# Three attention blocks on TensorE issued one projection unit later, each beside its neighbour (hybrid decoder layer, one core)

## The chip, the cores and the metric

The kernel runs on one core of one Trainium2 chip. The metric is the device time of one execution in microseconds (us), the median of several. PE is TensorE's matmul stream, PEld its weight loads, DVE VectorE, ACT ScalarE, POOL GpSimd, SP the engine that issues most of the DMAs.

## What is computed

One decoder layer over 512 positions of width 2048 in float32: RMSNorm, a combined input projection, two attention groups side by side, an output projection, then a SwiGLU feed-forward block and a final RMSNorm. Only the attention with the projections around it matters here:

```python
h = rmsnorm(x, attn_norm)
proj = einsum('bsd,de->bse', h, w_in)        # qa, ka, va (16 heads), qb (16 heads), kb, vb (2 kv heads)
out_a = dilated_attention(qa, ka, va)        # (window, dilation) = (128,1), (512,4), (2048,16), merged
out_b = swa_sink_attention(qb, kb, vb)       # window 128, learned sinks, 8 query heads per kv head
mix = concat(rmsnorm(out_a), rmsnorm(out_b))
x = x + mix @ w_out
x = x + (silu(h2 @ w_gate) * (h2 @ w_up)) @ w_down      # h2 = rmsnorm(x)
```

## The kernel before

Every engine runs its own instruction stream, written out by hand, and the streams meet only in counting semaphores. Float32 products are made of two fp32r halves: a tensor is split into a high part (ACT, `..._hi`) and the rest (DVE, `..._lo`), and three products of halves are added in PSUM.

**Units.** The projection is cut into units. A unit is one 128x512 tile of weights, times h, 12 matmuls of 512 columns (`tall_unit`, L445 to L447, in a loop of four). A pass `pair(p, ...)` has 16 units: four each for q, k, v of group A and q of group B of head pair p. Behind unit number s of the pass PE issues `attend(s, a, kv)`, a piece of the attention of the pair before (a = p - 1). So attention is laced into the projection, and a unit between two pieces is the time in which the other engines answer the first. There are 8 such interlaced passes: pair(1), a loop over pairs 2 to 4, a loop over pairs 5 to 7, and the output projection's first 16 units (`out_unit`, L489 to L491, also 12 matmuls each), which carries the attention of pair 7.

**Attention of a pair** has four heads, h = 0 and 1 of group A (dilated), h = 2 and 3 of group B. For each:
- `scores` (L592, L593) makes blocks of q times k. For a head of group A the last block, `S_A[3:]`, uses bank 2 again and so waits until ACT has read the first block (`exp_done`).
- DVE adds the bias and takes row minima (`lows`, L1307), ACT takes exponentials (`exps`, L848), DVE the reciprocals of the sums, POOL scales the rows.
- `turn_p(a, h, r)` (L608) transposes the probabilities of round r into the one bank BANK_PT. ACT takes their high part (`pt_high`, L860), DVE the low part (`pt_low`, L1259). As there is one bank, each `turn_p` waits until the round before has its low part (`pt_lo_done`).
- `weigh_v(a, h, r)` (L624, L625) multiplies round r with v into BANK_O. After a head's last round ACT copies one half of that bank (`o_lower`, L869), and DVE adds the two halves (`take_o`, L1334).
- `turn_v` (L632) transposes v for the pair.

Heads 0 and 1 have three rounds, heads 2 and 3 two. ACT and DVE step through the same 16 numbers: each first splits the weights three units ahead (`split`: w_hi L805 on ACT, w_lo L1250 on DVE; ACT's waits until the unit four before has been used), then does its own piece. At step 12 these pieces read, word for word:

```python
# ACT, attend(s, a)
            if s == 12:
                o_lower(a, 1)
                pt_high(a, 2, 0)
# DVE, attend(s, a)
            if s == 12:
                denominators(a, 3)
                take_o(a, 1)
                pt_low(a, 2, 0)
```

The low part's wait and the bank's wait are `pe.wait_ge(pt_lo_done, ROUNDS * a + r0 + r)` in `turn_p`, where r0 is 0, 3, 6, 8 for the four heads and ROUNDS is 10.

Of the kernel before, what the change touches and what calls it, by code (L numbers as in the profile page):

```python
# [99 lines left out]
def build(nc, x, x_turned, gain_cols, w_in, sinks, w_out, w_gate, w_up, w_down, final_norm, c_dist, c_lnm, c_band, c_slope, c_ident, x_mid, gu_mid, out):  # L100
# [341 lines left out]
    def _(pe):  # L442
# [143 lines left out]
        def scores(a, h, blocks):  # L586
            kind, odd, _ = HEAD[h]
            q, kh, kl = q_both[kind][odd], k_both[kind][odd], k_lo[kind][odd]
            for b, bk, c0, k0, keys, _ in blocks:
                qs, ks, s = slice(P * b, P * (b + 1)), slice(k0, k0 + keys), bank[bk][:, c0:c0 + keys]  # L590

                nc.tensor.matmul(s, q[:, qs], kh[:, ks], start=True, stop=False, skip_group_check=True)  # L592
                nc.tensor.matmul(s, q[:, qs], kl[:, ks], start=False, stop=True,  # L593
                                 skip_group_check=True).then_inc(s_ready, 1)

        def turn_p(a, h, r):

            kind, _, r0 = HEAD[h]
            if r == 0:
                pe.wait_ge(p_ready, 16 * a + 4 * (h + 1))  # L600
            if not (isinstance(a, int) and a == 0 and r0 + r == 0):
                pe.wait_ge(pt_lo_done, ROUNDS * a + r0 + r)
            where = E_A if kind == "A" else E_B
            for kb, qbs, c0 in (PT_A if kind == "A" else PT_B)[r]:
                for n, qb in enumerate(qbs):
                    e, k0 = where[qb]
                    e += P * kb - k0
                    mm = nc.tensor.transpose(bank[BANK_PT][:, c0 + P * n:c0 + P * (n + 1)],  # L608
                                             probs[h % 2][:, e:e + P], ident[:, :])
            mm.then_inc(pt_ready, 1)  # L610

        def weigh_v(a, h, r):

            kind, odd, r0 = HEAD[h]
            rounds = PT_A if kind == "A" else PT_B
            pe.wait_ge(pt_lo_done, ROUNDS * a + r0 + r + 1)
            if r == 0 and h > 0:
                pe.wait_ge(o_taken, 4 * a + h)
            buf = (r0 + r) % 2
            for i, (kb, qbs, c0) in enumerate(rounds[r]):  # L620
                n = P * len(qbs)
                v = v_both[kind][:, kb, 2 * odd:2 * odd + 2, :].rearrange("p a d -> p (a d)")
                o = bank[BANK_O][:, P * qbs[0]:P * qbs[0] + n]
                nc.tensor.matmul(o, v, pt_hi[:, buf, c0:c0 + n], start=r == 0 and i == 0, stop=False, skip_group_check=True)  # L624
                mm = nc.tensor.matmul(o, v, pt_lo[:, buf, c0:c0 + n], start=False,  # L625
                                      stop=r == len(rounds) - 1 and i == len(rounds[r]) - 1, skip_group_check=True)
            mm.then_inc(pv_done, 1)

        def turn_v():

            for t in range(NT):
                mm = nc.tensor.transpose(bank[BANK_O][:, P * t:P * (t + 1)], proj[0][:, P * t:P * (t + 1)], ident[:, :])  # L632
            return mm

        def attend(s, a, kv):

            first = isinstance(a, int) and a == 0
            if s == 0:
                pe.wait_ge(qa_lo_done, 2 * (a + 1))
                pe.wait_ge(ka_lo_done, 2 * (a + 1))  # L640
                pe.wait_ge(ka_hi_done, 4 * (a + 1))
                if first:
                    pe.wait_ge(k_rest_zero, 4)
                if not first:
                    pe.wait_ge(exp_done, 16 * a)
                scores(a, 0, S_A[:3])
            if s == 1:
                pe.wait_ge(exp_done, 16 * a + 1)
                scores(a, 0, S_A[3:])
            if s == 2:  # L650
                pe.wait_ge(acc_taken, 5 + 4 * a)
                if first:
                    pe.wait_ge(vb_all_done, 1)
                else:
                    pe.wait_ge(o_taken, 4 * a)
                turn_v().then_inc(vt_ready, 1)
            if s == 3:
                pe.wait_ge(exp_done, 16 * a + 4)
                scores(a, 1, S_A[:3])
            if s == 4:  # L660
                turn_p(a, 0, 0)
                pe.wait_ge(exp_done, 16 * a + 5)
                scores(a, 1, S_A[3:])
            if s == 5:
                turn_p(a, 0, 1)
                pe.wait_ge(va_lo_done, a + 1)
                weigh_v(a, 0, 0)
            if s == 6:
                turn_p(a, 0, 2)
                weigh_v(a, 0, 1)  # L670
                pe.wait_ge(qb_lo_done, 2 * (a + 1))
                pe.wait_ge(kb_lo_done, 2 * (kv + 1))
                pe.wait_ge(exp_done, 16 * a + 8)
                scores(a, 2, S_B)
            if s == 7:
                weigh_v(a, 0, 2)
            if s == 8:
                turn_p(a, 1, 0)
            if s == 9:
                turn_p(a, 1, 1)  # L680
                weigh_v(a, 1, 0)
                pe.wait_ge(exp_done, 16 * a + 12)
                scores(a, 3, S_B)
            if s == 10:
                turn_p(a, 1, 2)
                weigh_v(a, 1, 1)
            if s == 11:
                weigh_v(a, 1, 2)
                turn_p(a, 2, 0)
            if s == 12:  # L690
                turn_p(a, 2, 1)
            if s == 13:
                pe.wait_ge(vb_lo_done, 2 * (kv + 1))
                weigh_v(a, 2, 0)
                turn_p(a, 3, 0)
            if s == 14:
                weigh_v(a, 2, 1)
                turn_p(a, 3, 1)
            if s == 15:
                weigh_v(a, 3, 0)  # L700
                weigh_v(a, 3, 1)

        def pair(p, a, kv):

            for c, b in enumerate((BANK_Q, BANK_K, BANK_V, BANK_K)):

                if c == 0 and a is not None:
                    pe.wait_ge(acc_taken, 4 * p - 1)
                if c == 3 or c == 1 and a is not None:
                    pe.wait_ge(acc_taken, 4 * p + c + 1)  # L710
                if c == 2 and a is not None:
                    pe.wait_ge(acc_taken, 4 * p + 1)
                for j in range(4):
                    tall_unit(U_PAIR // 4 + 4 * p + c, j, b, h_hi, h_lo)
                    if a is not None:
                        attend(4 * c + j, a, kv)
                    if a is None and c == 1 and j == 2:
                        pe.wait_ge(ident_loaded, 16)
                        spread_r(squares[:, :].rearrange("p (t c) -> p t c", c=P), 1, BANK_PT)
                    if a is None and c == 2 and j == 0:  # L720
                        pe.wait_ge(acc_taken, 2)
                        turn_v().then_inc(vbt_ready, 1)
# [14 lines left out]
        for g in range(2):  # L737
            for s in range(16):
                out_unit(g, s)
                if g == 0:  # L740
                    attend(s, PAIRS - 1, 1)
                if g == 1 and s == 2:

                    pe.wait_ge(sq_added, 2 * PAIRS)
                    pe.wait_ge(pt_lo_done, ROUNDS * PAIRS)
                    for i, kind in enumerate("AB"):
                        for t in range(NT):
                            mm = nc.tensor.matmul(bank[BANK_PT][:, 4 * i + t:4 * i + t + 1],
                                                  sq_sum[kind][:, P * t:P * (t + 1)], ones[:, 0:1], start=True, stop=True)
                    mm.then_inc(ssq_ready, 1)  # L750
# [1128 lines left out]
```

## Time and profile before

| what | value |
|---|---|
| time, median of 3 runs | 2032.45 us (2032.43 to 2033.32) |
| the profiled execution's own time | 2031.41 us |
| its span, first to last instruction | 2029.6 us |
| PE busy | 2013.4 us, 99% of the span |
| DVE, ACT, POOL busy | 75%, 50%, 7% |
| mean granted clock of TensorE | 0.999 |

Durations below come from the profiled execution. A matmul's row shows when it starts and how long it lasts, fill and drain included; since matmuls overlap, what one costs in a stream is the distance from its start to the next one's start. "Idle before" in square brackets is the time that the engine stood empty ahead of an instruction, with the instruction that released it.

### The profile page before, as it was taken

What the parts mean: (1) busy time and instruction counts of PE and PEld (TensorE: products, weight loads), DVE (VectorE), ACT (ScalarE), POOL (GpSimd) and SP (SyncE); (2) the same over time, 40 slices, a digit from 0 to 9 for tenths busy, and PEclk for the clock granted to TensorE, in tenths of its full rate; (3) what the DMA queues carried; (4) which work ended last, traced back from release to release, by engine and by line L of the source; (5) the groups of instructions that cost most, each with busy time, mean ns of one, the idle gap of its engine ahead of it and who ended that gap; (6) DMA issues with size and microseconds to landing.
All of it is one profiled execution on the core that took longest, in us unless ns stands there. A gap on an engine that the chain in (4) does not pass through costs nothing.

```text
span 2029.6 us, 30889 instructions
## 1 busy us (share of the span) xinstructions
PE 2013.4 (99%) x10492; PEld 1721.1 (85%) x10492; DVE 1529.3 (75%) x2250; ACT 1005.9 (50%) x1874; POOL 142.4 (7%) x235
## 2 busy tenths in 40 slices
PE   9999999999999999999999999999999999999998
PEld 8888888887888988888888888888888888888886
DVE  5666666666766999899999999999998546546446
ACT  6455555554436654555555555554555323333333
POOL 0122222221100000000000000000000000000000
PEclk9999999999999999999999999999999999999999
DMA  8222222224234344444444444444447653544433
GB/s 295 83 77 70 77 72 73 73 72 153 76 99 154 117 139 137 126 139 127 139 138 136 134 136 134 128 142 132 130 139 244 239 180 100 176 155 119 140 96 132
DMA packets 263775, 265.32 MB, mean 131 GB/s; under 512 B 14081, under 2 KB 194561, under 8 KB 262657
## 3 DMA queue, kind: packets, MB, share of 16 engines
q1 hardware_dynamic: 249136, 224.97, 36.7%
q0 software_dynamic: 6336, 23.07, 2.9%
q10 hardware_dynamic: 8208, 15.98, 2.2%
q8 instruction: 65, 1.06, 0.2%
q14 instruction: 30, 0.24, 0.0%
HBM read 232.51 MB, written 31.46 MB: 130 GB/s over the span
## 4 chain that ended last, share of the span: by engine, by line
PE 78%; DVE 9%; issue 6%; ACT 4%; DMA 2%; SPq 0%; ACTq 0%; DVEq 0%; POOLq 0%; POOL 0%
PE bank L556 22%; PE bank L560 11%; PE bank L489 10%; PE bank L490 10%; PE bank L491 10%; PE bank L445 4%; PE bank L447 4%; PE bank L446 4%; DVE t_lo L1533 2%; ACT probs L848 1%; ACT w_hi L805 1%; DMA t_raw<-in_w_up 1%; PE bank L608 1%; DVE w_lo L1250 1%; DMA raw<-in_w_in 1%
## 5 line engine op out<-in xcount | busy, mean ns | idle before, releaser
L556 PE MATMUL bank<-s_two,t_hi 128*128 128x512 f32 x2352 | 609.9, 392 | 2.1 <-ACT part L1070 1.3
L1250 DVE TENSOR_TENSOR w_lo<-raw,w_hi 128x512 fp32r<-128x512 f32 x364 | 253.4, 698 | 381.6 <-ACT w_hi L805 379.6
L1030 ACT ACTIVATE t_hi<-t_raw 128x1792 fp32r<-128x1792 f32 x176 | 303.0, 1723 | 376.4 <-DVE t_raw L1527 221.6
L556 PEld LDWEIGHTS bank<-s_two,t_hi 128*128 128x128 f32 x2352 | 413.0, 188 | 66.5 <-issue 1.5
L805 ACT ACTIVATE w_hi<-raw 128x512 fp32r<-128x512 f32 x364 | 229.0, 631 | 479.4 <-PE bank L491 352.7
L560 PEld LDWEIGHTS bank<-s_two,t_lo 128*128 128x128 f32 x2352 | 338.2, 190 | 35.4
L1533 DVE TENSOR_TENSOR t_lo<-t_raw,t_hi 128x1792 fp32r<-128x1792 f32 x176 | 355.4, 2020 | 10.7 <-ACT t_hi L1030 10.5
L560 PE MATMUL bank<-s_two,t_lo 128*128 128x256 f32 x2352 | 347.6, 281 | 0.0
L489 PE MATMUL bank<-w_hi,down_hi 128*128 128x512 f32 x640 | 249.1, 389 | 0.4 <-DVE down_lo L1259 0.4
L491 PE MATMUL bank<-w_hi,down_lo 128*128 128x512 f32 x640 | 249.0, 389 | 0.0
L490 PE MATMUL bank<-w_lo,down_hi 128*128 128x512 f32 x640 | 249.0, 389 | 0.0
L1524 DVE TENSOR_TENSOR t_raw<-t_raw 128x1024 f32<-128x1024 f32 x176 | 214.9, 1221 | 33.1 <-DMA t_raw<-in_w_up 32.5
L445 PE MATMUL bank<-h_hi,w_hi 128*128 128x512 f32 x544 | 218.3, 401 | 1.1 <-DVE w_lo L1250 1.1
L447 PE MATMUL bank<-h_lo,w_hi 128*128 128x512 f32 x544 | 212.9, 391 | 0.0
L446 PE MATMUL bank<-h_hi,w_lo 128*128 128x512 f32 x544 | 212.7, 391 | 0.0
L489 PEld LDWEIGHTS bank<-w_hi,down_hi 128*128 128x128 f32 x640 | 120.2, 188 | 26.1 <-issue 1.2
L491 PEld LDWEIGHTS bank<-w_hi,down_lo 128*128 128x128 f32 x640 | 120.2, 188 | 24.9
L490 PEld LDWEIGHTS bank<-w_lo,down_hi 128*128 128x128 f32 x640 | 120.2, 188 | 24.7
L1070 ACT ACTIVATE part<-bank 128x256 f32<-128x256 f32 x294 | 123.2, 419 | 0.0
L447 PEld LDWEIGHTS bank<-h_lo,w_hi 128*128 128x128 f32 x544 | 102.1, 188 | 22.6
L1069 ACT ACTIVATE part_low<-bank 128x256 f32<-128x256 f32 x294 | 120.3, 409 | 0.5
L445 PEld LDWEIGHTS bank<-h_hi,w_hi 128*128 128x128 f32 x544 | 102.5, 188 | 20.0 <-DVE w_lo L1250 1.5
(170 smaller groups left out, 2506.9 us busy)
## 6 DMA issues: line engine op xcount, KB each, us to landing
raw<-in_w_down SPq DMA_DIRECT2D x176, 256.0 KB, 3.2
t_raw<-in_w_gate SPq DMA_DIRECT2D x174, 256.0 KB, 3.1
t_raw<-in_w_up SPq DMA_DIRECT2D x174, 256.0 KB, 3.4
raw<-in_w_in SPq DMA_DIRECT2D x136, 256.0 KB, 2.6
gu_s<-gu_mid SPq DMA_DIRECT2D x44, 512.0 KB, 5.3
gu_mid<-part POOLq DMA_DIRECT2D x43, 512.0 KB, 2.9
raw<-in_w_out SPq DMA_DIRECT2D x64, 256.0 KB, 3.2
x_row<-in_x ACTq DMA_DIRECT2D x4, 1024.0 KB, 12.4
```

The source lines that it names most:

```text
L445: nc.tensor.matmul(out_ap, st_hi, mv_hi, start=start, stop=False, skip_group_check=True)
L446: nc.tensor.matmul(out_ap, st_lo, mv_hi, start=False, stop=False, skip_group_check=True)
L447: return nc.tensor.matmul(out_ap, st_hi, mv_lo, start=False, stop=stop, skip_group_check=True)
L489: nc.tensor.matmul(b[:, :], ah[:, ts], w_hi[:, slot, :], start=first, stop=False, skip_group_check=True)
L490: nc.tensor.matmul(b[:, :], ah[:, ts], w_lo[:, slot, :], start=False, stop=False, skip_group_check=True)
L491: return nc.tensor.matmul(b[:, :], al[:, ts], w_hi[:, slot, :], start=False, stop=last, skip_group_check=True)
L556: nc.tensor.matmul(bank[SEVEN_BANK[i]][:, :], t_hi[r][:, SEVEN[i][0], q, :], both, start=d == 0 and q == 0, stop=False, skip_group_check=True)
L560: mm = nc.tensor.matmul(bank[SEVEN_BANK[i]][:, 0:HALF], t_lo[r][:, SEVEN[i][0], q, :], s_two[2 * d + q][:, SEVEN[i][1], 0, :], start=False ...
L805: nc.scalar.activation(w_hi[:, s, :], raw[:, s, :], ACT.Copy).then_inc(w_hi_done, 1)
L1030: nc.scalar.activation(t_hi[r][:, :, :, :].rearrange("p a q c -> p (a q c)"), t_raw[r][:, 1:8, :, :].rearrange("p a q c -> p (a q c)"), AC ...
L1250: nc.vector.tensor_tensor(w_lo[:, s, :], raw[:, s, :], w_hi[:, s, :].bitcast(F32), ALU.subtract).then_inc(w_lo_done, 1)
L1533: nc.vector.tensor_tensor(t_lo[r][:, :, :, :].rearrange("p a q c -> p (a q c)"), t_raw[r][:, 1:8, :, :].rearrange("p a q c -> p (a q c)"), ...
```

## The change

Three blocks on PE move behind the next unit, each to a place where PE already issued a block. No instruction is added, removed or altered, and ACT's, DVE's, POOL's and SP's streams are as before.

```diff
                 scores(a, 0, S_A[:3])
-            if s == 1:
+            if s == 2:
                 pe.wait_ge(exp_done, 16 * a + 1)
                 scores(a, 0, S_A[3:])
-            if s == 2:
                 pe.wait_ge(acc_taken, 5 + 4 * a)
...
-            if s == 7:
+            if s == 8:
                 weigh_v(a, 0, 2)
-            if s == 8:
                 turn_p(a, 1, 0)
...
-            if s == 11:
+            if s == 12:
                 weigh_v(a, 1, 2)
                 turn_p(a, 2, 0)
-            if s == 12:
                 turn_p(a, 2, 1)
```

The third join is seen in PE's stream at steps 11 and 12. Before, with unit 12 (L445 to L447) standing between the two rounds of transposes of head 2 (probs_94):

```order
L624 MATMUL bank<-pt_hi,vA_both 128x256 [waits pt_lo_done]
L625 MATMUL bank<-pt_lo,vA_both 128x256
L608 MATMUL bank<-ident,probs_94 128x128 [waits pt_lo_done,p_ready]
L608 MATMUL bank<-ident,probs_94 128x128 x3
L445 MATMUL bank<-h_hi,w_hi 128x512 [waits w_lo_done,acc_taken]
...
L608 MATMUL bank<-ident,probs_94 128x128 [waits pt_lo_done]
L608 MATMUL bank<-ident,probs_94 128x128 x2
L445 MATMUL bank<-h_hi,w_hi 128x512 [waits w_lo_done]
```

The same place of the changed kernel:

```order
L445 MATMUL bank<-h_hi,w_hi 128x512 [waits w_lo_done,acc_taken]
...
L624 MATMUL bank<-pt_hi,vA_both 128x256 [waits pt_lo_done]
L625 MATMUL bank<-pt_lo,vA_both 128x256
L608 MATMUL bank<-ident,probs_94 128x128 [waits pt_lo_done,p_ready]
L608 MATMUL bank<-ident,probs_94 128x128 x3
L608 MATMUL bank<-ident,probs_94 128x128 [waits pt_lo_done]
L608 MATMUL bank<-ident,probs_94 128x128 x2
L445 MATMUL bank<-h_hi,w_hi 128x512 [waits w_lo_done]
```

Unit 12 has moved ahead of the last weighing of head 1 and of the first four transposes; the second round's three transposes, with their wait on `pt_lo_done`, now follow the first round's four directly.

ACT's stream at its step 12 and the start of step 13, the same in both kernels but for line numbers (here of before):

```order
L805 ACTIVATE w_hi<-raw 128x512 [waits w_used,raw_loaded3]
L869 ACTIVATE o_low<-bank 64x512 [waits o_taken,pv_done]
L857 REGISTER_ALU
L860 ACTIVATE pt_hi<-bank 128x512 [waits pv_done,pt_ready]
...
L805 ACTIVATE w_hi<-raw 128x512 [waits w_used]
```

Nothing moves here: the copy of BANK_O's half (o_low, which waits for the weighing by `pv_done`) still stands ahead of the high part of the transposes (pt_hi).

The first join in PE's stream at steps 1 and 2. Before, the last scores of head 0 stand ahead of unit 2:

```order
L592 MATMUL bank<-kA_both_80,qA_both_76 128x256 [waits exp_done]
L593 MATMUL bank<-kA_lo_83,qA_both_76 128x256
L445 MATMUL bank<-h_hi,w_hi 128x512 [waits w_lo_done]
...
L632 MATMUL bank<-ident,proj_74 128x128 [waits vb_all_done,acc_taken]
L632 MATMUL bank<-ident,proj_74 128x128 x3
```

The changed kernel:

```order
L445 MATMUL bank<-h_hi,w_hi 128x512 [waits w_lo_done]
...
L592 MATMUL bank<-kA_both_80,qA_both_76 128x256 [waits exp_done]
L593 MATMUL bank<-kA_lo_83,qA_both_76 128x256
L632 MATMUL bank<-ident,proj_74 128x128 [waits vb_all_done,acc_taken]
L632 MATMUL bank<-ident,proj_74 128x128 x3
```

The two score matmuls have moved behind unit 2 and stand right ahead of the transposes of v.

## Rows read from the trace of the kernel before

**Rows 1.** The page, part 1 and part 2: PE busy, and its granted clock.

```profile
PE 2013.4 (99%) x10492; PEld 1721.1 (85%) x10492; DVE 1529.3 (75%) x2250; ACT 1005.9 (50%) x1874; POOL 142.4 (7%) x235
PEclk9999999999999999999999999999999999999999
```

**Rows 2.** Waits of PE from 76 to 540 us: total, times, longest.

```profile
PE bank L489 <- DVE y_a L1485: 1.3, 1, 1.3
PE bank L608 <- DVE pt_lo L1259: 1.2, 6, 0.4
PE bank L592 <- ACT probs L848: 1.0, 2, 0.6
```

**Rows 3.** Timeline of PE, one pass, steps 11 to 13: start, duration, instruction.

```profile
231.97 0.28 PE L624 MATMUL bank<-pt_hi,vA_both 128*128 128x256 f32 x1
232.09 0.28 PE L625 MATMUL bank<-pt_lo,vA_both 128*128 128x256 f32 x1
232.21 0.60 PE L608 MATMUL bank<-ident,probs 128*128 128x128 f32 x4
232.56 0.48 PE L445 MATMUL bank<-h_hi,w_hi 128*128 128x512 f32 x1
232.88 0.40 PE L446 MATMUL bank<-h_hi,w_lo 128*128 128x512 f32 x1
...
235.41 0.51 PE L608 MATMUL bank<-ident,probs 128*128 128x128 f32 x3
235.68 0.47 PE L445 MATMUL bank<-h_hi,w_hi 128*128 128x512 f32 x1
```

**Rows 4.** Timeline of ACT at the same step 12.

```profile
232.89 0.59 ACT L869 ACTIVATE o_low<-bank 64x512 f32<-64x512 f32 x1
233.50 0.60 ACT L860 ACTIVATE pt_hi<-bank 128x512 fp32r<-128x512 f32 x1
```

**Rows 5.** Timeline of DVE at the same step 12.

```profile
233.91 0.69 DVE L1334 TENSOR_TENSOR o_t<-bank,o_low 64x512 f32 x1
234.63 0.69 DVE L1259 TENSOR_TENSOR pt_lo<-bank,pt_hi 128x512 fp32r<-128x512 f32 x1
```

**Rows 6.** Timelines of PE and ACT, step 15: a weighing and its o_low.

```profile
537.05 0.28 PE L625 MATMUL bank<-pt_lo,vB_both 128*128 128x128 f32 x1
537.37 0.59 ACT L869 ACTIVATE o_low<-bank 64x512 f32<-64x512 f32 x1 [0.20 <-PE bank L625]
```

**Rows 7.** Timelines of ACT and DVE, step 14: a high and its low part.

```profile
239.64 0.60 ACT L860 ACTIVATE pt_hi<-bank 128x512 fp32r<-128x512 f32 x1 [0.28 <-PE bank L608]
240.27 0.69 DVE L1259 TENSOR_TENSOR pt_lo<-bank,pt_hi 128x512 fp32r<-128x512 f32 x1 [0.19 <-ACT pt_hi L860]
```

**Rows 8.** Timelines of ACT, DVE and PE, same pass, steps 8 and 9.

```profile
220.31 0.59 ACT L869 ACTIVATE o_low<-bank 64x512 f32<-64x512 f32 x1
221.53 0.67 DVE L1334 TENSOR_TENSOR o_t<-bank,o_low 64x512 f32 x1
222.13 0.14 DVE L1319 TENSOR_TENSOR den<-den,sink_exp 128x4 f32<-128x4 f32 x1
223.03 0.68 DVE L1259 TENSOR_TENSOR pt_lo<-bank,pt_hi 128x512 fp32r<-128x512 f32 x1
220.27 0.60 PE L608 MATMUL bank<-ident,probs 128*128 128x128 f32 x4
223.77 0.66 PE L608 MATMUL bank<-ident,probs 128*128 128x128 f32 x4 [0.17 <-DVE pt_lo L1259]
```

**Rows 9.** Timelines of PE and DVE, same pass, step 2.

```profile
198.71 0.60 PE L632 MATMUL bank<-ident,proj 128*128 128x128 f32 x4
199.37 0.43 DVE L1307 CUSTOM_DVE_ANT_0 bank<-bank,bias 128x256 f32<-128x256 f32 x1
```

**Rows 10.** Timeline of PE in the last interlaced pass, steps 1 and 4.

```profile
484.43 0.39 PE L592 MATMUL bank<-kA_both,qA_both 128*128 128x256 f32 x1 [0.56 <-ACT probs L848]
493.19 0.47 PE L489 MATMUL bank<-w_hi,act_hi 128*128 128x512 f32 x1 [1.32 <-DVE y_a L1485]
```

## The prediction, made before the changed kernel was run

> **What bounds the kernel now.** I read the page first: PE is busy 99% of the span at full granted clock, DVE 75%, ACT 50% [rows 1]. So the length is PE's stream plus the waits in it, and a gain elsewhere is worth nothing unless PE waited for it. Second, PE's waits in the eight interlaced passes, the only stretch in which the moved lines run: 1.3 us for DVE's copies of y_a, 1.2 us in six waits for a low part, 1.0 us in two waits for an exponential [rows 2]. That is 3.5 us of 464, and with what a wait costs beside its idle time (estimate: twice 0.06 each) at most some 5 us: all that a better order could win. Third, the timelines of PE, ACT and DVE of one pass, at each of the three joins. The reader is to see there which work of ACT and DVE answers a PE block and how long the answer takes, since a block that needs an answer and follows its question without a unit between waits for all of it.
>
> **What PE itself pays for order.** A unit that follows transposes starts slowly: its first matmul takes 0.32 us to the next (232.56 to 232.88), while the whole unit takes 2.85 us (232.56 to 235.41), so the other eleven take 0.23 each [rows 3]. A unit that follows nothing of the kind takes 2.76. Everything is issued as often as before, so apart from waits the moves change PE by less than 0.1 us for each run of transposes that is cut or joined.
>
> **Join 3 (step 12), the one that costs.** Before, the first round of head 2 (four transposes at 232.21) and the second round (235.41) have unit 12 between them [rows 3]. They share one bank, and the second waits for the low part of the first. After, the second follows directly, so PE waits for the round trip: ACT's copy and high part, DVE's sum and low part. I take T as the start of the weighing behind unit 12. In the pass shown, unit 12 would start where the weighing did, at 231.97, and take 2.76, so T = 234.73. From T:
> - The weighing's second matmul starts 0.12 later and lasts 0.28 (232.09, 0.28): T + 0.40 [rows 3].
> - ACT's step 12 begins with o_low, which needs that weighing. Its lag behind PE is 0.04: a weighing that ends at 537.33 releases it at 537.37 [rows 6]. ACT is free by then: its split of unit 15 waits for unit 11 alone and was over when o_low started at 232.89 [rows 4]. o_low starts at T + 0.44, and pt_hi 0.61 behind it (232.89 to 233.50) at T + 1.05 [rows 4]; the four transposes, 0.24 to 0.84 behind T, are over [rows 3].
> - DVE's step 12 has the sum o_t ahead of pt_lo. o_low lasts 0.59, and I take 0.03 from ACT's end to DVE's start, as from pt_hi (239.64 + 0.60) to pt_lo (240.27) [rows 7]: o_t at T + 1.06. pt_lo starts 0.72 behind o_t (233.91 to 234.63) and lasts 0.69 [rows 5]: T + 1.78 to T + 2.47. By ACT alone it could have started at T + 1.05 + 0.60 + 0.03 = T + 1.68, so DVE's sum ends last, by 0.1.
> - PE starts again 0.06 later: pt_lo ends at 223.71, the transposes start at 223.77 [rows 8]. T + 2.53.
>
> Without the wait the second round would start at T + 0.24 + 0.35 = T + 0.59 [rows 3]. The three transposes then take 0.27 to the next unit (235.41 to 235.68) [rows 3], plus 0.06 for a restart, since the four behind a wait last 0.66 where others last 0.60 [rows 8]. Unit 13 starts at T + 2.86 = 237.59, and it started at 235.68: **1.91 us more for each pass**. The saved slow start of unit 12 is in this already. With eight passes: 15.3 us. ACT and DVE have each the same instructions there, one unit later; while PE waits they can run ahead by no more than the weights they split (three units), so nothing is earned with the time.
>
> Behind the waiting transposes stand unit 13 and all later units; ACT's split of unit 16 waits for unit 12 only and fills the wait; DVE's take of v comes at T + 2.4 and is needed only at step 2 of the next pass; the second round's high and low parts follow the transposes as before and unit 13 covers them.
>
> How much DVE's hand-over is worth is the one unsure term. Behind head 1's o_t the next instruction starts 0.72 later, after its end [rows 5]; behind head 0's it starts 0.60 later, ahead of its end (221.53 to 222.13) [rows 8]. I take the first, since join 3 has head 1's: 1.91 a pass. With 0.60, DVE would be ready at T + 1.66, ACT's path (T + 1.68) would end last, and the pass would lose 1.81, 14.5 us in all. The page "VectorE: DVE Perf Modes" of the Trainium skill (section "Two Vector instructions with no wait between them") has a rule that tells the two apart: an instruction is held until all earlier ones are finished when its operands start in another group of 32 partitions than theirs did. Head 1's sum lies in partitions 64 to 127 and pt_lo starts at 0, head 0's starts at 0. By that rule the hold comes with join 3 in every pass, which is the 15.3 and not the 14.5; the two distances agree with it.
>
> **Join 2 (step 8), nothing.** The weighing of head 0's last round now ends just ahead of the transposes at 220.27, at about 220.27 - 0.12 + 0.28 = 220.43. o_low started at 220.31 and now starts at 220.47, 0.16 later. DVE takes o_t at 221.53, behind other work; o_low would be done at 221.06. So pt_lo stays at 223.03 and the transposes behind it at 223.77 [rows 8]. The cover is DVE's queue, 0.47 us of it; if that were gone, the wait at 223.77 would grow by at most the 0.16 us, 1.3 us over eight passes.
>
> **Join 1 (step 2), nothing.** The last scores of head 0 come one unit later and end right ahead of turn_v at 198.71, by about 198.71 + 0.16 = 198.87. DVE reads them at 199.37, behind the low part of q and a split [rows 9], so 0.5 us of cover is left. Where PE waited there for the exponential, that wait goes: in the last pass 0.56 us at 484.43. But 9 us later PE waits 1.32 us for DVE's y_a, whose start DVE's own queue sets, and time won at 484 is waited off at 493.19 [rows 10]. I take 0; the bounds are a gain of 0.6 us, and a loss of 0.5 us for each pass (4 us) if DVE got there earlier than in the rows.
>
> **Sum.** The profiled execution took 2031.41 us (span 2029.6); + 15.3 = 2046.7. The median of the runs shown is 1.04 us above the profiled one, so 2032.45 + 15.3 = 2047.8 us.
>
> **Bounds of the wait.** Low: the 14.5 above, less 0.6 from join 1: 2046. Lower still if the wait's restart costs nothing and lags are shorter by 0.1: 2045. High: lags of 0.1 more at each of four hand-overs: 2.3 a pass, 18.5: 2051.
>
> **The rivals.**
> - *The joins 1 and 2 cost as well* (6%). DVE's queue between steps 2 and 8 decides PE's wait at 223.77; it has 0.5 us of cover at either join. If the moved blocks come too late in most passes, up to 0.5 us each are added: 2047.8 + 4 to 8 = 2052 to 2056. For it: the wait there exists already in six passes, so there is no slack on PE's side. Against: the two covers above.
> - *The clock falls* (3%). PE stands empty for 1.7 us once a pass (from T + 0.84 to T + 2.53). In the trace the longest wait of these passes is 1.32 us, with the granted clock at full behind it [rows 1, 10], so 1.7 is not far outside what is seen. If one unit of each pass then ran at 1.2 instead of 2.4 GHz, its 2.76 us would double: 22 us more, 2070. The page "TensorE: Matmul & The Clock Gate" of the Trainium skill (Part 1) states that an array left idle has its clock halved until work has warmed it again; by it the rival's 2070 can come, and no row of this trace shows such a fall.
> - *The change does nothing* (5%). The second round's wait would have to be met already, for example if ACT and DVE ran their step 12 within the time of the weighing and the four transposes. They need 2.5 us where PE gives 0.6, so this asks for most of my chain to be wrong: 2032.
> - *Faster* (2%), the other side. One mechanism: where PE waits at steps 1, 5 and 9 (2.2 us in all, rows of the low parts and exponentials [rows 2]) the new order lets ACT and DVE catch up during the new wait and these go: up to 5 us off with restarts. It decides only if the wait of join 3 is under 0.3 us; each further 0.1 us costs 0.8. It would give 2028. Against: DVE's work of steps 2 to 8 answers PE blocks of the same pass, so a head start at step 12 of the pass before doesn't reach it.
>
> **Chances and range.** 84% for the forecast with its bounds of 2045 to 2051; the rivals 6, 3, 5 and 2%. The range 2043 to 2052 leaves out these and a little of the forecast's own spread. A difference of 0.2% (4 us) is about what a measurement tells from none: slower 0.93, same 0.05, faster 0.02.
>
> **What would show it.** In the changed kernel's profile: a new wait of PE, bank L605 (the transposes' line, three up) for pt_lo, eight more times, near 1.7 us each and 13 to 14 us in total, with PE's busy time unchanged within 1 us; DVE's o_t and pt_lo back to back in it; the waits at step 9 still near 0.17 us; the granted clock at 1.00; and unit 13 starting about 2.9 us behind the weighing of join 3. I am wrong if that wait is missing or under 1.2 us, if the waits at step 9 grow, or if matmuls behind the wait stand 0.46 us apart.

## The result, and the profile after

The changed kernel takes 2048.65 us (median of 5, 2047.96 to 2049.27), the kernel before 2032.45: ratio 1.0079, interval 1.0069 to 1.0090. That is 16.2 us slower, where 15.3 were forecast. The profiled execution has a span of 2047.4 us, 17.8 more than that of before.

The page of the changed kernel, the lines of [rows 1]:

```profile
PE 2015.7 (98%) x10492; PEld 1723.4 (84%) x10492; DVE 1534.2 (75%) x2250; ACT 1005.5 (49%) x1874; POOL 142.8 (7%) x235
PEclk9999999999999999999999999999999999999999
```

PE does the same work in 2.3 us more busy time, 1.6 of it in matmuls at the lowered clock described below; the rest of the 17.8 is waiting. Its waits from 76 to 560 us (total, times, longest), to be held against [rows 2]:

```profile
PE bank L608 <- DVE pt_lo L1256: 15.9, 14, 1.8
PE bank L489 <- DVE y_a L1482: 2.2, 1, 2.2
```

The transposes wait 14 times instead of 6: eight new waits of 14.2 us together, and the six old ones at step 9, which are now 0.24 instead of 0.17 (one 0.46 instead of 0.40). (Their line stands ahead of the diff and is still 608; I had written 605.) The wait for y_a has grown from 1.3 to 2.2, and the two waits for an exponential are gone. Step 12 of one pass, timelines of PE, ACT and DVE in turn (start, duration, instruction, idle before):

```profile
239.29 0.28 PE L624 MATMUL bank<-pt_hi,vA_both 128*128 128x256 f32 x1
...
239.53 0.60 PE L608 MATMUL bank<-ident,probs 128*128 128x128 f32 x4
241.93 0.55 PE L608 MATMUL bank<-ident,probs 128*128 128x128 f32 x3 [1.80 <-DVE pt_lo L1256]
242.23 0.48 PE L445 MATMUL bank<-h_hi,w_hi 128*128 128x512 f32 x1
...
239.73 0.59 ACT L866 ACTIVATE o_low<-bank 64x512 f32<-64x512 f32 x1 [2.26 <-PE bank L625]
240.34 0.60 ACT L857 ACTIVATE pt_hi<-bank 128x512 fp32r<-128x512 f32 x1
...
240.46 0.69 DVE L1331 TENSOR_TENSOR o_t<-bank,o_low 64x512 f32 x1 [1.98 <-ACT o_low L866]
241.18 0.69 DVE L1256 TENSOR_TENSOR pt_lo<-bank,pt_hi 128x512 fp32r<-128x512 f32 x1
```

This is the forecast chain, link by link, with T = 239.29: o_low at T + 0.44, pt_hi at T + 1.05, o_t at T + 1.17 (forecast 1.06), pt_lo at T + 1.89 (1.78), the transposes at T + 2.64 (2.53). ACT had stood idle for 2.26 us and DVE for 1.98 before it: both were free, and the answer could not come sooner because its question was asked so late.

In the first pass and the last the sum starts sooner behind the copy. The first pass, ACT and DVE:

```profile
121.05 0.59 ACT L866 ACTIVATE o_low<-bank 64x512 f32<-64x512 f32 x1 [2.26 <-PE bank L625]
121.67 0.69 DVE L1331 TENSOR_TENSOR o_t<-bank,o_low 64x512 f32<-64x512 f32 x1 [1.87 <-ACT o_low L866]
```

The other place that changed is the last pass. The timeline of PE around its wait for y_a, and windows (us, busy PE, granted clock, DMA share, GB/s) ahead of it, in it, and behind it:

```profile
507.49 0.47 PE L489 MATMUL bank<-w_hi,act_hi 128*128 128x512 f32 x1 [2.20 <-DVE y_a L1482]
507.80 0.59 PE L490 MATMUL bank<-w_lo,act_hi 128*128 128x512 f32 x1
508.19 0.63 PE L491 MATMUL bank<-w_hi,act_lo 128*128 128x512 f32 x1
508.61 0.63 PE L489 MATMUL bank<-w_hi,act_hi 128*128 128x512 f32 x1
509.04 0.63 PE L490 MATMUL bank<-w_lo,act_hi 128*128 128x512 f32 x1
...
511.17 0.44 PE L489 MATMUL bank<-w_hi,act_hi 128*128 128x512 f32 x1
```

```profile
485.00:505.00 20.00, 20.00 (x101) 1.00 0.58 194
505.00:507.40 2.40, 0.29 (x3) 1.00 1.05 397
507.80:511.00 3.20, 3.20 (x9) 0.51 0.70 252
512.00:520.00 8.00, 8.00 (x46) 1.00 0.26 76
```

Behind the wait of 2.20 us the granted clock falls to half (1.2 GHz) and stays there from about 507.8 to 511.2: matmuls of 512 columns stand 0.43 us apart instead of 0.23. From y_a to the next transposes PE takes 4.42 us (507.49 to 511.91) where it took 2.82 (493.19 to 496.01).

This is the profiled execution, whose mean granted clock is 0.998; that of the kernel before is 0.999. Of the five timed executions of the changed kernel three read 0.998 and two 0.999, so the fall may not come in every one of them.

### The profile page after: what moved, and what is told of

The parts are those of the page before. It is cut to its first block, busy times and chain, and to the rows that moved or that the text cites. A ratio compares the mean times of both kernels' runs of the same rounds, so it can differ in the third digit from the quotient of the medians.

```text
span 2047.4 us, 30889 instructions
## 1 busy us (share of the span) xinstructions
PE 2015.7 (98%) x10492; PEld 1723.4 (84%) x10492; DVE 1534.2 (75%) x2250; ACT 1005.5 (49%) x1874; POOL 142.8 (7%) x235
## 3 DMA queue, kind: packets, MB, share of 16 engines
q8 instruction: 65, 1.06, 0.2%
## 4 chain that ended last, share of the span: by engine, by line
PE 83%; DVE 6%; issue 5%; ACT 4%; DMA 1%; DVEq 0%; ACTq 0%; SPq 0%; POOLq 0%; POOL 0%
PE bank L556 24%; PE bank L560 12%; PE bank L489 10%; PE bank L490 10%; PE bank L491 10%; PE bank L445 5%; PE bank L447 5%; PE bank L446 5%; ACT probs L845 1%; ACT w_hi L802 1%; PE bank L608 1%; DVE t_lo L1530 1%; DVE pt_lo L1256 1%; DVE w_lo L1247 1%; PE bank L625 1%
## 5 line engine op out<-in xcount | busy, mean ns | idle before, releaser
L1247 DVE TENSOR_TENSOR w_lo<-raw,w_hi 128x512 fp32r<-128x512 f32 x364 | 259.1, 714 | 378.7 <-ACT w_hi L802 376.7
L445 PE MATMUL bank<-h_hi,w_hi 128*128 128x512 f32 x544 | 217.3, 399 | 1.6 <-DVE w_lo L1247 1.4
L447 PE MATMUL bank<-h_lo,w_hi 128*128 128x512 f32 x544 | 212.8, 391 | 0.0
L445 PEld LDWEIGHTS bank<-h_hi,w_hi 128*128 128x128 f32 x544 | 102.4, 188 | 21.8 <-DVE w_lo L1247 2.1
L447 PEld LDWEIGHTS bank<-h_lo,w_hi 128*128 128x128 f32 x544 | 102.1, 188 | 22.1
```

The source lines that it names most:

```text
L445: nc.tensor.matmul(out_ap, st_hi, mv_hi, start=start, stop=False, skip_group_check=True)
L447: return nc.tensor.matmul(out_ap, st_hi, mv_lo, start=False, stop=stop, skip_group_check=True)
L1247: nc.vector.tensor_tensor(w_lo[:, s, :], raw[:, s, :], w_hi[:, s, :].bitcast(F32), ALU.subtract).then_inc(w_lo_done, 1)
```

## The experiments

Each is an edit of the kernel before. Passes are measured from one turn_v to the next; in the kernel before a pass that is a copy of its neighbours takes 57.42 to 57.46 us, in the changed kernel 59.36 to 59.41. The mean of the first six such distances goes from 57.49 to 59.42, 1.93 more. "Before" was run again beside each group of kernels, so the ratios count and not the medians alone.

**Join 3 alone** (the third hunk of the diff).

> Join 3 alone (joins 1 and 2 left as before). Theory A, the round trip of join 3 is the change: eight new waits of PE of 1.7 to 1.8 us, the waits at step 9 at 0.17 as before, the last pass's wait for y_a at 1.3 and no fall of the clock; 8 x 1.93 = 15.4 us, so 2047.9 us, ratio 1.0076. Rival B, joins 1 and 2 carry a good part of the 16.2 us: under 2045.

Measured: 2048.65 us, ratio 1.0072 (1.0058 to 1.0085). Passes take 59.38. The waits of PE, against [rows 2]:

```profile
PE bank L608 <- DVE pt_lo L1258: 15.5, 14, 1.8
PE bank L592 <- ACT probs L847: 2.0, 2, 1.6
PE bank L489 <- DVE y_a L1484: 1.3, 1, 1.3
```

Eight waits of 1.69 to 1.80 are new, those at step 9 stay at 0.17 to 0.19 (one 0.43), the wait for y_a stays and the clock holds. The wait at step 1 of the last pass is 1.59 instead of 0.56; it differs that much between kernels without join 1 (see the run with the late loads), so this 1 us is not put down to join 3. Join 3 carries the change; rival B falls.

**Joins 1 and 2 alone** (the first two hunks).

> Joins 1 and 2 alone. Theory A: no wait at join 3; the waits at step 9 at 0.24 instead of 0.17 (+ 0.5 us over six passes); in the last pass PE comes 0.8 us earlier to the wait for y_a, which grows from 1.3 to about 2.2 us, the clock falls behind it (+ 1.6) and the later wait for an exponential goes (- 0.7): together + 1.4, 2033.9 us. Rival B: 2036 or more. Rival C, the joins are free and the fall of the clock needs join 3 as well: 2032.5 with the granted clock at 1.00 throughout.

Measured: 2033.8 us, ratio 1.0001 (0.9992 to 1.0010). Passes take 57.42. The waits at step 9 are 0.22 instead of 0.17, but passes are no longer, and the wait for y_a is 1.95. Its line, and windows of PE from it on:

```profile
493.42 0.47 PE L489 MATMUL bank<-w_hi,act_hi 128*128 128x512 f32 x1 [1.95 <-DVE y_a L1483]
493.00:494.50 1.50, 1.08 (x5) 1.00 1.05 388
494.50:497.50 3.00, 2.55 (x15) 1.00 0.75 255
```

The granted clock stays at full behind that wait (these windows are the same as in the next run, with the clock in the column behind the count). The forecast of + 1.4 was too high: what it charged for the fall did not come in this execution, nor did the later wait for an exponential go (0.45). The time is rival C's, but its condition, that the fall needs join 3, is refuted by the next run. And the trace is one execution: of the 11 that were timed four read a mean granted clock of 0.998 or 0.997, and they took 2034.05 to 2036.64 us, where this one reads 0.999 and took 2032.77.

**Join 1 alone**, and **join 2 alone**.

> Join 1 alone. Theory: only the last pass changes; the wait for the exponential at step 1 goes, the wait for y_a grows to about 2.2 us, the granted clock falls to 0.5 for about 3 us behind it, the wait at step 4 goes: + 0.9, 2033.4 us; the waits at step 9 stay at 0.17. Rival: join 1 shifts DVE's queue, so that the waits at step 9 grow to 0.24.

> Join 2 alone. Theory: o_low starts 0.15 us later and pushes ACT's split, which DVE's order covers; the waits at step 9 grow to 0.24 or stay at 0.17 (whichever join does it shows it here or in join 1 alone): 2032.5 to 2033.0 us. The last pass as before.

Measured: join 1, 2035.02 us, ratio 1.0005 (0.9996 to 1.0015); join 2, 2034.49 us, ratio 1.0002 (0.9993 to 1.0011). Passes take 57.40 in both. With join 1 the waits at step 9 are 0.17 to 0.19, with join 2 0.15 to 0.16 (in both kernels but for the one long wait of 0.40 and 0.42), so neither does alone what the two do together, and all of it is below 0.1 us. Join 1 alone has a wait for y_a of 2.24, and there the clock fell:

```profile
494.01 0.76 PE L489 MATMUL bank<-w_hi,act_hi 128*128 128x512 f32 x1 [2.24 <-DVE y_a L1484]
493.00:494.50 1.50, 0.49 (x1) 0.71 1.04 384
494.50:497.50 3.00, 3.00 (x9) 0.58 0.56 202
```

From y_a to the next transposes join 1 alone takes 4.25 us (494.01 to 498.26), joins 1 and 2 took 2.80 (493.42 to 496.22). The one has lost the clock behind 2.24 us, the other kept it behind 1.95. Why the two waits differ is open. Of the ten timed executions of join 1 alone five read 0.998. A reading under 0.999 is on record for no execution of a kernel without join 1, the late weighing below excepted: join 1 is what brings the fall, though not shown in every execution.

**Only the last weighing of head 1 later**; head 2's first transposes stay ahead of unit 12.

```diff
             if s == 11:
-                weigh_v(a, 1, 2)
                 turn_p(a, 2, 0)
             if s == 12:
+                weigh_v(a, 1, 2)
                 turn_p(a, 2, 1)
```

> Only the last weighing of head 1 moves behind unit 12; the four transposes of head 2's first round stay ahead of unit 12. Theory A in detail (ACT's copy of the weighing's result stands ahead of the high part in ACT's queue, DVE's sum ahead of the low part): ACT waits for the weighing, so the low part comes 2.5 us behind the weighing as in join 3, while PE wants it after 0.24: waits of 2.1 us, about 2.3 us a pass, 18.5 in all, 2051 us. Rival D, what costs is that the two rounds of transposes stand side by side with no unit between: unit 12 is between them here, so 2032.5.

Measured: 2065.32 us, ratio 1.0157 (1.0142 to 1.0173), 14 us slower than theory A had it. The timeline of PE in one pass:

```profile
180.60 0.28 PE L624 MATMUL bank<-pt_hi,vA_both 128*128 128x256 f32 x1
180.71 0.28 PE L625 MATMUL bank<-pt_lo,vA_both 128*128 128x256 f32 x1
183.24 0.55 PE L608 MATMUL bank<-ident,probs 128*128 128x128 f32 x3 [2.24 <-DVE pt_lo L1259]
183.54 0.50 PE L445 MATMUL bank<-h_hi,w_hi 128*128 128x512 f32 x1
183.86 0.61 PE L446 MATMUL bank<-h_hi,w_lo 128*128 128x512 f32 x1
184.26 0.63 PE L447 MATMUL bank<-h_lo,w_hi 128*128 128x512 f32 x1
184.69 0.63 PE L445 MATMUL bank<-h_hi,w_hi 128*128 128x512 f32 x1
...
187.50 0.39 PE L446 MATMUL bank<-h_hi,w_lo 128*128 128x512 f32 x1
```

And its windows there:

```profile
184.00:187.00 3.00, 3.00 (x9) 2.32 (x8) 1.66 (x2) 0.31 (x1) 0.64 (x1) 0.50 0.21 34
```

The wait is near the forecast of 2.1 (2.24, or 2.13 in the first and last pass), although unit 12 stands between the two rounds of transposes: rival D falls. What is unforecast is the clock, at 0.50 behind each of these waits but the first. A middle pass takes about 61.40, 3.97 more: 1.6 for the matmuls at half clock (the twelve of the unit stand 4.19 us from first to last instead of 2.60) and the other 2.4 for the wait and its restart.

**The same, with ACT's and DVE's step 12 in the other order.**

```diff
 # ACT
-                o_lower(a, 1)
                 pt_high(a, 2, 0)
+                o_lower(a, 1)
 # DVE
-                take_o(a, 1)
                 pt_low(a, 2, 0)
+                take_o(a, 1)
```

> As the run before, but at step 12 ACT takes the high part ahead of the copy, and DVE the low part ahead of the sum. Theory A: high and low part are done during unit 12, no wait is left at the second round, 2032.5 us (within 1). Rival D: the same 2032.5. If the wait stays at 2 us, the order of ACT's and DVE's queues was not what held it and theory A's chain is wrong.

Measured: 2033.1 us, ratio 0.9997 (0.9987 to 1.0006); passes that are copies of each other take 57.3 to 57.5. ACT and DVE, same step:

```profile
233.28 0.58 ACT L860 ACTIVATE pt_hi<-bank 128x512 fp32r<-128x512 f32 x1
236.13 0.59 ACT L869 ACTIVATE o_low<-bank 64x512 f32<-64x512 f32 x1 [2.27 <-PE bank L625]
```

```profile
234.30 0.69 DVE L1259 TENSOR_TENSOR pt_lo<-bank,pt_hi 128x512 fp32r<-128x512 f32 x1
236.86 0.69 DVE L1334 TENSOR_TENSOR o_t<-bank,o_low 64x512 f32 x1 [1.87 <-ACT o_low L869]
```

High and low part are done during unit 12, and the copy and the sum follow the weighing, needed by nobody for one more unit. All 32 us of the run before are gone with two pairs of lines changing places: there it was not PE's order alone but its mismatch with ACT's and DVE's.

**Join 3 alone, with ACT and DVE in the other order.**

> Join 3 alone, with ACT's high part ahead of its copy and DVE's low part ahead of its sum at step 12. Theory A: the chain is then transposes, high part, low part: T + 0.84 + 0.04 + 0.60 + 0.03 + 0.69 + 0.06 = T + 2.26 instead of T + 2.53 to 2.64, waits of 1.4 to 1.5 us, 1.66 us a pass, 13.3 in all, 2045.7 us. If the copy and the sum had nothing to do with it: as join 3 alone.

Measured: 2047.13 us, ratio 1.0061 (1.0046 to 1.0076); passes take 59.0. PE, ACT and DVE:

```profile
238.88 0.60 PE L608 MATMUL bank<-ident,probs 128*128 128x128 f32 x4
240.89 0.55 PE L608 MATMUL bank<-ident,probs 128*128 128x128 f32 x3 [1.41 <-DVE pt_lo L1258]
239.51 0.60 ACT L859 ACTIVATE pt_hi<-bank 128x512 fp32r<-128x512 f32 x1 [2.70 <-PE bank L608]
240.14 0.69 DVE L1258 TENSOR_TENSOR pt_lo<-bank,pt_hi 128x512 fp32r<-128x512 f32 x1 [2.32 <-ACT pt_hi L859]
240.87 0.70 DVE L1333 TENSOR_TENSOR o_t<-bank,o_low 64x512 f32 x1
```

The wait is 1.41 in all eight passes and a pass loses 1.57 (forecast 1.66) instead of 1.94. So of join 3's price a fifth is the copy and the sum ahead in the queues; four fifths are transposes, high part, low part in a row. No order of ACT and DVE can remove these while both rounds share one bank and no unit lies between; that is argued from the waits in the code, not tested with a second bank. The medians of the two join 3 runs are from different groups; the passes of their traces are what tells them apart.

**DVE's low part ahead of its split at step 9**, in the kernel before.

```diff
 # DVE, pair() and the last pass
             for s in range(16):
+                if s == 9:
+                    pt_low(a, 1, 0)
                 split(*ahead(...))
...
-            if s in (9, 10, 11):
+            if s in (10, 11):
                 pt_low(a, 1, s - 9)
```

In the last pass the added line asks for `g == 0` too, the first 16 units.

> Half of the run with the late loads: DVE's low part at step 9 ahead of its split, the loads of x left where they were. Theory: passes of 57.05 us instead of 57.43 in the six that waited; 2.3 us, 2031 to 2030 us, ratio 0.9989; the last pass's three waits as before.

Measured: 2030.76 us, ratio 0.9988 (0.9979 to 0.9997). The six waits at step 9 are gone and passes take 57.1. The last pass keeps its waits:

```profile
PE bank L489 <- DVE y_a L1487: 1.3, 1, 1.3
PE bank L592 <- ACT probs L848: 0.8, 2, 0.4
```

**The same, and in the last pass ACT issues its loads of x later.** Ahead of the exponentials of step 1 stood four DMA issues.

```diff
-                    if s == 1:
-                        for n in range(NC):
-                            act.dma_start(x_mix[n][:, :, :], ...)
                     attend(s, PAIRS - 1)
+                    for n in {6: (0, 1), 10: (2, 3)}.get(s, ()):
+                        act.dma_start(x_mix[n][:, :, :], ...)
```

> No join. DVE takes the low part at step 9 ahead of its split, and in the last pass ACT issues its four loads of x after steps 6 and 10 instead of ahead of the exponentials of step 1. Theory: each wait of PE in the passes has its cause in an in-order queue in front of the answer. The six waits at step 9 go (0.32 us each, 0.55 once: 2.1 us), and with the exponentials 2 us earlier in the last pass the waits of 0.56, 1.32 and 0.43 us go too (2.6 with restarts): 2027.8 us, ratio 0.9977. If the loads now come late for what uses them, a new wait stands in the next 16 units.

Measured: 2030.8 us, ratio 0.9985 (0.9976 to 0.9994), two thirds of the gain that was expected; the expected 0.9977 lies just inside the interval, so it is the trace that decides. No new wait stands in the next 16 units. The wait at step 1, which was anything from 0.37 to 1.59 us in the kernels that issue the loads ahead of it and lack join 1, is gone; the other two stand nearly as they were:

```profile
PE bank L489 <- DVE y_a L1485: 1.0, 1, 1.0
PE bank L592 <- ACT probs L848: 0.4, 1, 0.4
```

I had counted all three waits as one cause, and two of them do not hang on the loads. My reading is that the chain behind y_a begins earlier, but PE does too, and DVE's own work of steps 2 and 3 lies between; the next run tests that work.

**And DVE's bias of head 1 behind the copies of y_a.**

```diff
+            last = isinstance(a, int) and a == PAIRS - 1
...
-                set_bias(a, 1)
+                if not last:
+                    set_bias(a, 1)
             if s == 4:
+                if last:
+                    set_bias(a, 1)
```

> The run with both edits, and in the last pass DVE sets head 1's bias after the copies of y_a and its next split instead of ahead of them. Theory, as for join 1 in the last pass (time won ahead of a wait that another queue sets is waited off there): the wait of 1.01 for y_a shrinks to 0.1, the wait of 0.42 behind it for an exponential grows by the same 0.9, since DVE's next row minima start no earlier; within 0.3 us of the run with both edits. Rival: 0.9 us faster.

Measured: 2029.49 us, ratio 0.9980 (0.9971 to 0.9989). One wait is left in the passes:

```profile
PE bank L592 <- ACT probs L848: 1.2, 1, 1.2
```

As forecast, the wait for y_a went and the one behind it grew by 0.8. Two waits have become one and little is won by it; whether this kernel is faster than the one before it in the list the intervals don't tell. It is the fastest median of the study and beats both kernels of the case, the original by 0.2% (0.1 to 0.3).

## Why the prediction was right, step by step

- **Join 3 costs the round trip: shown.** Alone it gives 1.0072 of the change's 1.0079. Forecast per pass 1.91, measured 1.93 (means 57.49 and 59.42). That it is so close is luck: the wait is 1.80 where I had 1.7, while unit 12 without transposes ahead took 2.72 (236.57 to 239.29) where I had 2.76, and unit 13 followed 0.30 behind the waiting transposes (241.93 to 242.23) where I had 0.33.
- **The mis-sized term** is the hand-over from ACT to DVE's o_t, for which I took 0.03 from another pair of instructions [rows 7]. It is 0.14 in the six middle passes (239.73 + 0.59 to 240.46) and 0.03 in the first (121.05 + 0.59 to 121.67) and last, whose waits are 1.70 and 1.69. The middle passes are loops, in which o_t is addressed through a register. The runs agree: with the low part, which has no such address, at the head of DVE's step, the wait is 1.41 in all eight; and o_t is 0.14 behind its copy in the late weighing with the other order as well (236.13 + 0.59 to 236.86). That the address is the cause was not tested apart.
- **DVE's 0.72 behind head 1's o_t: as taken** (240.46 to 241.18). The rule that I cited from "VectorE: DVE Perf Modes" of the Trainium skill agrees in the other order too: in join 3 with ACT and DVE swapped, o_t changes the partitions back and starts 0.73 behind pt_lo (240.14 to 240.87). This run and the changed kernel show the hold; none shows head 1's sum without it.
- **Join 2 free: right** within what the traces show (pass 57.40, wait at step 9 at 0.15).
- **Two of the stated signs did not come out.** I had written that I am wrong if the waits at step 9 grow: they grew from 0.17 to 0.24 in the changed kernel, and to 0.22 with joins 1 and 2 alone, where passes are no longer (57.42). The sign was too strict, since a wait can grow by what PE saves ahead of it; which work moves it is open. And PE's busy time rose by 2.3 us where I allowed 1, mostly by the lowered clock.
- **Join 1 free in the loops: right. In the last pass: half right.** As forecast, the time won at step 1 was waited off at y_a: turn_v came 0.8 us less late than join 3's price has it, and y_a's wait grew by 0.88. I stopped there and did not ask what 2.2 us of emptiness does to the clock: in the profiled execution it cost 1.60 us, of which 0.69 came back, since ACT had meanwhile caught up with the exponential of step 4 (from the transposes to the next unit 0.68 us, 511.91 to 512.59, where it was 1.37, 496.01 to 497.38).
- **The clock as a rival** came true at a place where I had not looked for it. I had priced it for join 3's waits of 1.7 us, and behind all of those the clock stays at full. I had also priced a fall at a whole unit, 2.76 us; the three kernels whose profiles show one paid 1.45 to 1.6 us for each. The page "TensorE: Matmul & The Clock Gate" of the Trainium skill (Part 1) has the mechanism. The trace agrees that an array left idle loses half its clock and gets it back while it works: 0.51 from 507.80 to 511.00, and 1.00 from 512.00 on.
- **The sum.** Between the two profiled executions lie 17.8 us: 0.7 at the start ahead of the first pass, 12.7 up to the last pass's turn_v, 3.7 in the last pass (0.88 + 1.60 - 0.69 + 1.9), and 0.7 in the stages behind, where nothing was changed and the kernels of this study differ by up to 3 us among each other (waits for t_lo of 0.2 to 2.3 us in all are part of it). So about 1.4 us of the profiled difference, and some of the median's, is not the change's. Those differences I did not explain. That 15.3 came so near to the 16.2 of the medians rests on join 3; the last pass's own costs were not in my sum.

## What to carry to other kernels

When a block is moved towards its neighbour on the engine that sets the time, ask for each wait in the neighbour which block it answers: if that is the one just moved next to it, the whole round trip becomes idle time, whatever is saved by joining. Before moving a question later, look at what stands ahead of the answer in the queues of the engines that answer; two lines there decided between 0 and 32 us. And a wait that absorbs time won elsewhere can grow until the clock falls behind it: here PE won about 0.8 us ahead of the wait for y_a, and where the clock fell that cost 1.45 to 1.6 us.

## What the runs showed of the hardware beyond the expected

- In the profiled executions the granted clock held at 1.00 behind waits of PE of 1.41, 1.80 and 1.95 us, was at half behind 2.20 and 2.24, and did either behind 2.13: not in the first pass of the late-weighing run, but in the last (matmuls 0.43 us apart from 556.18 on). The same kernel can do either from one execution to the next, as the mean clocks of 0.999 to 0.997 with joins 1 and 2 alone suggest; only the profiled one can be looked into.
- A fall cost 1.45 us in join 1 alone (4.25 against 2.80), 1.60 in the changed kernel and about 1.6 in a pass of the late weighing, where it came on top of 2.4 for the wait itself.
- An answer from PE through ACT to DVE and back costs 2.0 us for a 128x512 block (238.88 to 240.89), although the two instructions on the way last 0.60 and 0.69; the rest is the 0.60 that the four transposes last by their row, and three hand-overs of 0.03 to 0.06.
